# Queries' halves before the weight casts, last mixing and last down projection by token tile, and one weight booked into another buffer

## The reference

```python
# first part, layer 1: attention B, whose queries come from the same normed x as keys and values
kv = rms_norm(x, kv_norm_g) @ kv_w
q = (rms_norm(x, mix_pre_g[1]) @ b_w_q)
...
# second part, last layer
mods = split(silu(c) @ w_ada + b_ada, 9)               # 18 column groups of 512
mixed = sigmoid(ga) * (y_a @ w_a) + sigmoid(gb) * (y_b @ w_b)
h = h + mods[5] * (mixed @ w_out)                      # "last mixing", names lo
hn = rmsnorm(h, g_ffn2) * (1 + mods[7]) + mods[6]      # names nl, l
a, b = split(hn @ w_ffn2_in, 2)
h = h + 0.5 * mods[8] * ((silu(a) * b) @ w_ffn2_out)   # down projection, names ld
return rmsnorm(h, g_final)
```

## Time and profile before

| what | value |
| --- | --- |
| median of 3 runs | 1660.45 us |
| the profiled execution, its own time | 1659.65 us |
| its span, first to last instruction | 1657.8 us |
| mean granted TensorE clock | 0.995 of full speed |
| busy: PE, DVE, ACT, POOL | 98%, 59%, 50%, 9% |

### The profile page before, as it was taken

The page is one execution under the profiler, slowest core; times in us unless marked ns, Lnnn a source line. Parts: engine busy times, 40 slices in busy tenths (PEclk is TensorE's granted clock), DMA queues, the critical chain, the costliest instruction groups (busy, mean ns, idle before and its releaser), DMA issues.

```text
span 1657.8 us, 25510 instructions
## 1 busy us (share of the span) xinstructions
PE 1623.1 (98%) x10737; PEld 1450.4 (87%) x10737; DVE 980.9 (59%) x1652; ACT 827.1 (50%) x1188; POOL 149.4 (9%) x141
## 2 busy tenths in 40 slices
PE   7999999999999999999999999999999999999997
PEld 6888899987879989998899999889888888689985
DVE  5676744445635575446665666557747876655444
ACT  4575544434569754444454465444545546354442
POOL 1210000100002200111001100001000000001000
PEclk9999999999999999999999999999999999999999
DMA  9756866776663355556555676588572565665552
GB/s 325 240 203 220 273 219 227 239 242 240 213 200 102 123 194 180 178 180 214 190 171 166 197 142 190 178 174 174 137 157 70 136 163 178 202 217 178 178 171 84
DMA packets 224417, 309.46 MB, mean 187 GB/s; under 512 B 5004, under 2 KB 146720, under 8 KB 224304
## 3 DMA queue, kind: packets, MB, share of 16 engines
q1 hardware_dynamic: 222064, 301.29, 59.6%
q0 software_dynamic: 1664, 5.84, 1.0%
q10 hardware_dynamic: 576, 0.71, 0.1%
HBM read 306.77 MB, written 1.05 MB: 186 GB/s over the span
## 4 chain that ended last, share of the span: by engine, by line
PE 88%; DVE 6%; ACT 3%; issue 1%; DMA 0%; POOL 0%; DVEq 0%; ACTq 0%
PE ps L144 86%; PE ps L147 2%; DVE wl L157 2%; DVE SM L167 1%; DVE MT L167 1%; ACT L153 1%; ACT wh L153 1%; ACT SA L153 1%; DVE X L167 0%; ACT FT L153 0%; DVE MT L164 0%; DMA X<-in_x_dram 0%; DVE XTL L157 0%; ACT MT L153 0%; DVE SA L167 0%
## 5 line engine op out<-in xcount | busy, mean ns | idle before, releaser
L157 DVE TENSOR_TENSOR wl<-raw,wh 128x1024 fp32r<-128x1024 f32 x498 | 607.5, 1259 | 410.3 <-ACT wh L153 409.5
L153 ACT ACTIVATE wh<-raw 128x1024 fp32r<-128x1024 f32 x498 | 501.9, 1052 | 230.9 <-PE ps L144 106.4
L144 PE MATMUL ps<-XTH,wh 128*128 128x256 f32 x1792 | 515.6, 288 | 4.9 <-issue 3.6
L144 PE MATMUL ps<-XTH,wl 128*128 128x256 f32 x1792 | 507.6, 283 | 0.6 <-DVE wl L157 0.6
L144 PE MATMUL ps<-XTL,wh 128*128 128x256 f32 x1792 | 507.6, 283 | 0.0
L144 PEld LDWEIGHTS ps<-XTH,wh 128*128 128x128 f32 x1792 | 344.1, 192 | 17.6 <-issue 8.8
L144 PEld LDWEIGHTS ps<-XTL,wh 128*128 128x128 f32 x1792 | 344.1, 192 | 2.8 <-issue 2.4
L144 PEld LDWEIGHTS ps<-XTH,wl 128*128 128x128 f32 x1792 | 344.2, 192 | 0.8 <-DVE wl L157 0.8
L144 PE MATMUL ps<-wh,XTH 128*128 128x512 f32 x352 | 140.9, 400 | 0.0
L144 PE MATMUL ps<-wh,HTH 128*128 128x512 f32 x352 | 139.3, 396 | 0.0
L144 PE MATMUL ps<-wl,HTH 128*128 128x512 f32 x352 | 138.9, 395 | 0.0
(11 more groups left out here) (295 smaller groups left out, 2005.5 us busy)
## 6 DMA issues: line engine op xcount, KB each, us to landing
raw<-in_w_ffn_in_dram SPq DMA_DIRECT2D x66, 1024.0 KB, 5.1
raw<-in_ffn_w_gate_up_dram SPq DMA_DIRECT2D x44, 1024.0 KB, 5.1
raw<-in_w_in_dram SPq DMA_DIRECT2D x40, 1024.0 KB, 8.6
raw<-in_w_ada_dram SPq DMA_DIRECT2D x36, 1024.0 KB, 5.5
raw<-in_w_ffn_out_dram SPq DMA_DIRECT2D x30, 1024.0 KB, 5.1
raw<-in_ffn_w_down_dram SPq DMA_DIRECT2D x20, 1024.0 KB, 5.1
raw<-in_a_w_qkv_dram SPq DMA_DIRECT2D x12, 1024.0 KB, 7.3
raw<-in_kv_w_dram SPq DMA_DIRECT2D x8, 1024.0 KB, 5.9
```

What stands on the lines that cost most here:

```text
L144: return NOTHING if self.e is None else self.e.matmul(o, l, r, start=start, stop=stop, skip_group_check=skip)
L153: return self.e.activation(o, i, fn, bias=bias, scale=scale)
L157: return NOTHING if self.e is None else self.e.tensor_tensor(o, a, b, f)
```

## The change

It has four parts. (1) Behind `bv` the step that makes `XTH` and `XTL` is now ahead of the casts that were due. (2) The last mixing runs tile 0 to its end, then tile 1 (`by_tile`, for three of the four pieces); each tile has its own norm: tile 0's wholly on VectorE, tile 1's shared by columns; tile 0's eight transposes stand ahead of `products(16)`, tile 1's between the two halves of `products(17)`. (3) g0 is booked between the halves of `products(16)`, one place earlier in the loads. (4) The last two row groups of the down projection run by tile, and the final norm is made tile by tile, the last one for half the columns on each of two engines.

```diff
+            def by_tile(name, wt, plan, o, XH, XL, nk, ready):
+                parts = [(n0, kts, piece(wsrc(wt, kts[0], len(kts), n0, 512), len(kts), 512)[1]) for n0, kts in plan]
+                for t in range(2):
+                    for q, (n0, kts, gs) in enumerate(parts):
+                        sums((name, n0), gs, [(i, t) for i in range(len(gs))], kts, o[n0], XH, XL, nk, ready)
+                        GROUP[name, n0] = gs[-1]
+                        if kts[-1] == nk - 1:
+                            give((name, t, n0), v_out, name, t, n0)
...
             def block2_ffn(n, w_in, w_out, first):
                 if not first:
-                    own_first[0] = held[0] = True
+                    o = [take(n, "tr", kp) for kp in range(4)]
+                    turn_tile(n, 0, o, lambda k: v_norm.at("nl", 0))
+                    own_first[0] = True
                     yield "last", 1
+                    held[0] = True
                     yield "last", 2
-                to_halves(n, blocks_of(YF), normed_ready("n" + n), shifted=True)
+                    turn_tile(n, 1, o, lambda k: (a_norm if k < 4 else v_norm).at("nl", 1))
+                else:
+                    to_halves(n, blocks_of(YF), normed_ready("n" + n), shifted=True)
                 held[0] = False
-                yield ("gap", 1) if first else None
+                yield ("gap", 1) if first else ("last", 1)
...
+                    plan = [(n0, list(range(*ks))) for n0 in (0, 512) for ks in ((16, 20), (20, 22))]
+                    yield from by_tile("ld", w_out, plan, o, HTH, HTL, NF, hidden_ready(n))
...
-                    own_first[0] = q >= 2
+                    own_first[0] = held[0] = q == 2
+                own_first[0] = True
...
             def products(n):
                 for half in range(2):
+                    if half == 1 and n == 16:
+                        booked["l", "g", 0] = piece(wsrc(I["w_ffn2_in_2"][0], 0, 8, 0, 256), 8, 256)
+                    if half == 1 and n == 17:
+                        yield 0
...
-                if n == 16:
-                    booked["l", "g", 0] = piece(wsrc(I["w_ffn2_in_2"][0], 0, 8, 0, 256), 8, 256)
...
+            def tile_norm(name, x, Y, done_by):
+                next_after(dve.dot(small(S_MAIN, 1), Y[:, 0, :], x[:, 0, :], x[:, 0, :]))
+                rstd(S_MAIN + 4, small(S_MAIN, 1), 1, D, (name, "r", 0))
+                dve.ts(Y[:, 0, :], x[:, 0, :], small(S_MAIN + 6, 1), ALU.mult).then_inc(*v_norm.up(name, 0))
+
+            def tile_root(name):
+                s1 = small(S_MAIN + 1, 1)
+                next_after(dve.tt(s1, s1, small(S_MAIN + 2, 1), ALU.add))
+                rstd(S_MAIN + 8, s1, 1, D, (name, "r", 1))
...
-            for q in range(2):
-                sp.wait_ge(*v_norm.at("end", 0, q))
+            for t, q in ((0, 0), (0, 1), (1, 0)):
+                sp.wait_ge(*v_norm.at("end", t, q))
```

More of the change, by code:

```diff
@@ L942, in main @@
                 o = {n0: [take("lo", t, n0) for t in range(2)] for n0 in (0, 512)}
[L943 to L946, removed]
-                    yield 0
[L948 to L958, removed]
+                moving(("lo", 0), I["w_out_2"][0], 0, 0, list(range(4)), o[0], XUH, XUL, 8, half_ready("hw"))
+                to_halves("hw", blocks_of(GBB), lambda t, k: v_out.at("mix", t, 512), range(2, 4))
+                yield 0
+                plan = [(512, list(range(4))), (0, list(range(4, 8))), (512, list(range(4, 8)))]
+                for _ in by_tile("lo", I["w_out_2"][0], plan, o, XUH, XUL, 8, half_ready("hw")):
+                    yield 0
+                    own_first[0] = True
                 yield from block2_ffn("l", I["w_ffn2_in_2"][0], I["w_ffn2_out_2"][0], False)
@@ L990, in ada @@
                 for n in range(18):
-                    products(n)
+                    yield from products(n)
                     yield 0
@@ L1407, in block2_ffn @@
                     yield
-                yield from rows(NF, nothing)
+                if n == "e":
+                    yield from rows(NF, nothing)
             def main():
@@ new lines, in main @@
+                yield from block2_ffn("l", 6)
+                for _ in range(9):
+                    yield
+                act.wait_ge(*v_out.at("ld", "x", 0))
+                act.wait_ge(*g_out.at("ld", "x", 0))
+                act.act(YF[:, 0, :], X[:, 0, :], ACT.Square, acc=small(S_MAIN, 1)).then_inc(*a_norm.up("end", "sq", 0))
+                yield
+                act.wait_ge(*g_out.at("ld", "x", 1))
+                act.act(YF[:, 1, 0:512], X[:, 1, 0:512], ACT.Square, acc=small(S_MAIN + 1, 1))
@@ L2049, in block2_ffn @@
                     yield
-                yield from rows(NF, gated(n + "d", GB, "g" + n, X, MT))
+                if n == "e":
+                    yield from rows(NF, gated(n + "d", GB, "g" + n, X, MT))
             def branch_b(t, n0):
@@ L2210, in main @@
-                dve.wait_ge(*v_out.at("lo", "x", 1))
-                dve.wait_ge(*g_out.at("lo", "x", 1))
-                yield from block2_ffn("l", "g_ffn2_2", 6, "g5")
-                dve.wait_ge(*v_out.at("ld", "x", 1))
-                dve.wait_ge(*g_out.at("ld", "x", 1))
+                tile_norm("nl", X, YF, "lo")
+                evict(1, 0)
+                yield
+                evict(1, 512)
+                yield
+                yield from block2_ffn("l", "g_ffn2_2", 6, "g5")
+                for _ in range(8):
+                    yield
@@ L2368, in block2_ffn @@
                 yield from hidden(n, MT, HTH, HTL, range(11), 0)
-                yield from rows(NF, gated(n + "d", X, MT))
+                if n == "e":
+                    yield from rows(NF, gated(n + "d", X, MT))
             def main():
@@ L2446, in main @@
                 yield
+                evict = gated("lo", X, MT)
+                evict(0, 0)
                 yield
-                evict = gated("lo", X, MT)
-                for t in range(2):
-                    evict(t, 0)
-                    yield
+                evict(1, 0)
+                yield
+                yield
                 pool.wait_ge(*done("lo", 512))
@@ L2454, in main @@
                 yield from block2_ffn("l")
+                for _ in range(8):
+                    yield
+                evict = gated("ld", X, MT)
+                evict(0, 0)
+                yield
+                evict(1, 0)
+                yield
+                yield
             def spatial():
@@ L2467, in ada @@
                 pool.dma(WG[:, :, :], win[:, 3072:3088].rearrange("(k p) n -> p k n", p=P)).then_inc(*d_wg.up("wg"))
-                for n in range(5):
+                for n in range(6):
                     yield
```

124 lines of the change are left out of this document (83 added, 41 removed).

## The result

The changed kernel takes 1662.44 us (median of 20 runs, 1661.71 to 1663.55), the kernel before 1658.94 us on the same chip (20 runs, 1658.09 to 1660.75). The ratio is 1.0019, with a 95% interval of 1.0012 to 1.0026: slower by 3.1 us (0.19% of 1659); the two medians lie 3.5 us apart. That is at the edge of the 0.2% (3.3 us) that was called no change, and small as it is, the interval leaves no doubt that the kernel is slower. The prediction was 1661.7 us, +1.2 us, in a range of 1656.9 to 1665.9. One execution of the filler experiment took 4132 us and is left out of its ratio; nothing here shows why it did.

What follows compares the result with a forecast made beforehand. The prediction took TensorE, busy for 98% of the span, to bound the kernel. Its terms, -4.0 - 3.3 + 8.4 + 1.7 - 1.6 = +1.2 us on the median 1660.45, gave 1661.7 us, range 1656.9 to 1665.9.

Steps and rivals of the forecast that it cites:

- The mechanism: Behind g0, g1's cast waits for its load and holds AT in ScalarE's first-in-first-out queue; TensorE stands 9.6 us.
- forecast of no change that could be told: Whole kernel: time within 0.2%, 3.3 us, of the kernel before, between 1657.1 and 1663.8 us; chance 0.62.
- queries' halves: At the query products: XTH and XTL start earlier, TensorE waits 2.5 us less, group at full clock; -4.0 us.
- tile 1's norm: At the last norm, behind the mixing: earlier last sum, shorter square and root, earlier transposes, g0 starts at 1451.1; -3.3 us.
- wait for g1: Behind g0: g1's load is issued only at g0's end, so TensorE waits 9.6 us instead of 1.2; +8.4 us.
- clock behind it: Behind the wait after g0: TensorE falls to half clock from standing; +1.7 us, between 0 and twice that.
- end: From the last down-projection product to the span's end: shorter square and root -0.95, one scaling per engine -0.7; -1.6 us.
- the rival of a gain that doesn't last: At the attention behind the queries: the 4.0 us gain is lost; sum +5.2, 1665.7 us; chance 0.08.
- a query group that starts later than 473: At the queries' halves: sign that the prediction is wrong if TensorE starts the group after 473; 472.3 was expected.
- then g0's two subtractions, 2.4 us: On VectorE at the last mixing: both subtractions take 2.4 us between tile 1's gated products; last sum ends at 1444.6.
- the rival of a late landing: Behind g0: the first two loads share the transfer evenly, g1 lands 3.4 us later; sum +4.6, 1665.1 us; chance 0.12.
- that of a hidden wait: Behind g0: AT doesn't stand behind g1's cast, or g1's load lands before g0 ends; -8.9 us, 1651.6 us; chance 0.07.

Runs made afterwards that it cites:

- the filler experiment: The changed kernel with 76 extra matmuls of 256 columns on TensorE ahead of the columns of AT: 1660.56 us, ratio 1.0006 to the kernel before.
- the second execution of the old code: Profiled execution of the kernel before with only the queries' halves moved; its last norm is unchanged code, and g0 started 10.65 us behind the mixing.
- The seventh experiment: The changed kernel with tile 1's first sum into X at the mixing on VectorE instead of GpSimd: 1661.92 us, ratio 1.0019 to the kernel before.
- the first: The changed kernel with g1's two casts and subtractions placed behind AT in ScalarE's and VectorE's queues: 1651.29 us, ratio 0.9952 to the kernel before.
- fourth experiments: The kernel before with only the queries' halves put ahead of the casts: 1655.11 us, ratio 0.9975 to the kernel before.
- third: The kernel before with only g0's weight booked one place earlier, ahead of the second half of products(16): 1669.77 us, ratio 1.0063.
- ninth experiments: The changed kernel with TensorE's columns of AT moved from behind g0 to behind g1: 1652.17 us, ratio 0.9954 to the kernel before.

## Why the prediction came out as it did

The mechanism was right, with a wait of 9.75 us where the change put it. The forecast of no change that could be told, by its own bound of 3.3 us, held by a hair: 3.1 us by the ratio, 3.5 by the medians, and an interval that leaves out 1. Of the +3.1 us, 1.2 were predicted.

That the forecast of 1661.7 us lies only 0.7 from the measured 1662.44 is luck. It was worked out on a median of 3 runs, 1660.45, and the kernel before measured 1658.94 in 20 runs, 1.5 less; this hid most of the 1.9 us by which the change itself was put too low. Within the change, too, an end that was put 0.6 too small made up for a part of what the other terms missed. Term by term, in the profiled pair:

| term | predicted | measured | by itself |
|---|---|---|---|
| queries' halves | -4.0 | -3.7 (-2.86 less 0.8) | -4.1 |
| tile 1's norm | -3.3 | -2.2 (-1.35 against the second execution of the old code) | not run |
| wait for g1 | +8.4 | +8.6 | |
| clock behind it | +1.7 | +2.5 (1.2 to 2.5 in four) | wait and clock: +10.5 |
| end | -1.6 | -2.2 | -3.3, undone |
| sum | +1.2 | +3.0 | |

**Queries' halves.** Right, and it stays to the end, so that the rival of a gain that doesn't last is out. The first product came at 472.46 in the time of before (473.27 - 0.8) for the 472.3 of the prediction, and the group took 6.17 us for 6.0. One of the prediction's own signs of being wrong, a query group that starts later than 473, is met by the letter, at 473.27. It was badly chosen: in the ten profiled executions with these halves moved the group starts between 472.48 and 473.48, always 0.22 us behind TensorE's coming free, so that the wait would have been the sign, and not the start.

**Tile 1's norm.** This is the step that was off by most: "then g0's two subtractions, 2.4 us". They took 3.45, since GpSimd's sum into X runs beside them. The last sum into X ended 2.8 us behind the mixing, for the 1.7 of the prediction, and that is the 1.1 by which g0 started late against the forecast (9.3 us behind the mixing for 8.2). The seventh experiment shows it: with GpSimd off they take 2.36. The trace of before had a row of it that I didn't weigh: the X add of GpSimd at the mixing also took 2.19 us there (at 1441.88), beside VectorE's sum of squares (1.22 us), against 1.29 for tile 0's. The remaining steps came nearly as worked out: last sum to root 0.8 us (1442.93 to 1443.72), root 2.2 for 1.9 (1443.72 to 1445.89), the transposes 0.8 behind it for 0.8 (the prediction's 1447.4 for the root's end adds up to 1447.3), MT 0.5 behind them for 0.6, g0 2.3 behind MT. A second thing was read and not weighed: the transposes of before stood 0.8 us late because `products(17)` ran at half clock, so that 0.8 of the 3.3 us of gain were that execution's; the same code ran without it in the execution with the queries' halves alone. The part has no run by itself. Norm and end together are -3.9 us by the first and fourth experiments (-8.0 less -4.1) and -4.4 in the profiled pair; the ratios' intervals are too wide to divide that further.

**Wait for g1.** Each piece came as the rows of before gave it: 5.3 us from g0's end to the cast (5.2), 2.0 for two casts (1.95), 1.3 for the table load, 0.5 to AT, 0.65 to TensorE. The three loads behind each other did not share the transfer: issued at 1456.66, 1457.07 and 1457.69, they landed 5.2, 7.8 and 10.2 us later, some 3 us apart, so the rival of a late landing is out, and so is that of a hidden wait; the first, third and ninth experiments say from three sides that it is the order in ScalarE's queue that makes the late load dear.

**Clock.** The size was right for the mean of four executions, 1.8; the profiled pair has one at the long end. The range given, 0 to 3.4, held. The term was taken over from a stand of 2.58 us to one four times as long; that the size fitted was not argued for and is partly luck.

**End.** The square and root gave 0.83 us for 0.95. From the final scaling to the span's end it took 3.7 us (1658.01 to 1661.7) instead of 5.1 (1652.70 to 1657.8): 1.4 saved for the 0.7 of the prediction. Half of that is the one scaling instead of two, as predicted; the rest lies behind the last issue (2.9 us from 1658.76 to the span's end, for some 3.7 before), where two outputs are under way instead of four. No run took that apart. Undone by itself the end cost 3.3 us in the timing, with an interval wide enough for 2.2.

The pieces run by themselves are consistent: -8.0 us for the changed kernel without the wait (0.9952) and +10.5 for the booking make +2.5, in the interval of the measured ratio (2.0 to 4.3 us). The 0.1 us in the middle and the 0.8 ahead of the first changed place lie within what these two stretches vary by over the twelve profiled executions (1.0 us up to the queries, 1.45 in the middle); what makes an execution late there stays open.

## What to carry to other kernels

In an engine's in-order queue an early place for a load's consumer is only harmless while the load is early: when a slot is booked differently, look up which piece's release now starts each of the next loads, and move the casts of the one that became late behind whatever the critical engine waits for. The change's three gains, 8 us in the traces, were real and were paid for by one order of two casts; moved, they gave all of it back (-8.0 us by the ratio). Where an operation with two inputs is priced from its mean, look whether another engine's sum runs beside it at that place.

## What was not expected of the hardware

- VectorE and GpSimd held each other up when both had two inputs in SBUF: 3.45 against 2.36 us for two 128x1024 subtractions of VectorE, 2.21 against 1.30 us for one 128x512 sum of GpSimd. Of the two subtractions only the second was longer (2.32 against 1.22 us).
- The cost of the half clock behind the same wait of 9.7 us was not the same from one execution to the next: 1.2, 1.6, 1.9 and 2.5 us. The granted clock was back at 1.00 between 2.4 us (the window 1465.49 to 1467.90 at 0.50, with GpSimd's sum on VectorE) and 5.7 us behind the first new work.
- A stand of 3.15 us ahead of AT, with the booking put back, was enough for half clock in the transposes and in the start of g0 (eight transposes in 1.97 us); one of 1.28 us at the same place in the changed kernel was not (1.09). Between them it went either way: behind a stand of 2.4 us at this place the same code ran `products(17)` at half clock in the kernel before and at full clock with the queries' halves alone (3.56 and 1.92 us), so that a gain read from one pair of traces can hold or lack 0.9 us.
